# Gate/up seven-product units: two block sums made by accumulating transfers on GpSimd's queue

## What is computed

```python
def _swiglu_ffn(x, norm_g, w_gate, w_up, w_down):
    h = _rmsnorm(x, norm_g)
    return (jax.nn.silu(h @ w_gate) * (h @ w_up)) @ w_down
```

## Time and profile before

| what | value |
|---|---|
| runs | 2599.98 us median (2594.21 to 2600.82) |
| span of the profiled execution, first to last instruction | 2591.4 us, 8.6 us below the median of the runs |
| TensorE busy | 2562.1 us, 99% |
| VectorE busy | 1954.8 us, 75% |
| ScalarE busy | 1339.8 us, 52% |
| GpSimd busy | 189.2 us, 7% |
| moved by DMA | 548.21 MB, 212 GB/s over the span |
| TensorE's granted clock | 0.999 of full speed |

### The profile page before, as it was taken

How to read it: one execution, slowest core, us unless ns; L and a number is a source line. 1 busy time by engine, 2 the same in 40 slices (tenths; PEclk the granted TensorE clock), 3 DMA queues, 4 the chain that set the end, 5 groups by cost and what they waited for, 6 DMA issues and landing times.

```text
span 2591.4 us, 34224 instructions
## 1 busy us (share of the span) xinstructions
PE 2562.1 (99%) x13659; PEld 2103.4 (81%) x13659; DVE 1954.8 (75%) x2311; ACT 1339.8 (52%) x1568; POOL 189.2 (7%) x346
## 2 busy tenths in 40 slices
PE   8999999999999999999999999999999999999998
PEld 7888888888888777878788888888888888888887
DVE  6888888887767796959666766555668888888876
ACT  5555555555556366446455544433455455555554
POOL 2000000000000011010001112000100000000000
PEclk9999999999999999999999999999999999999999
DMA  6767676667776575656488779643767677766655
GB/s 213 232 210 242 210 236 218 217 208 228 216 210 195 184 228 159 179 165 181 146 280 257 252 245 281 201 155 130 239 190 230 222 226 225 227 219 218 210 201 175
DMA packets 278576, 548.21 MB, mean 212 GB/s; under 512 B 25020, under 2 KB 35424, under 8 KB 278032
## 3 DMA queue, kind: packets, MB, share of 16 engines
q1 hardware_dynamic: 253904, 478.60, 58.3%
q0 software_dynamic: 24192, 66.89, 8.8%
q10 hardware_dynamic: 320, 0.53, 0.1%
HBM read 508.15 MB, written 37.77 MB: 211 GB/s over the span
## 4 chain that ended last, share of the span: by engine, by line
PE 86%; DVE 8%; ACT 3%; DMA 2%; issue 1%; POOL 0%; SPq 0%; DVEq 0%; ACTq 0%; POOLq 0%
PE pp L794 14%; PE pp L795 14%; PE pp L796 14%; PE pp L415 11%; PE pp L416 11%; PE pp L417 11%; DVE wlo L376 2%; PE pa L794 1%; PE pb L796 1%; PE pb L795 1%; PE pb L794 1%; PE pa L795 1%; PE pa L796 1%; ACT whi L371 1%; DMA raw<-in_ffn_w_up 1%
## 5 line engine op out<-in xcount | busy, mean ns | idle before, releaser
L376 DVE TENSOR_TENSOR wlo<-raw,whi 128x1024 fp32r<-128x1024 f32 (+1 forms) x764 | 919.6, 1216 | 345.9 <-ACT whi L371 326.2
L371 ACT ACTIVATE whi<-raw 128x1024 fp32r<-128x1024 f32 (+1 forms) x764 | 798.0, 1053 | 626.5 <-PE pp L417 438.1
L794 PE MATMUL pp<-whi,xhi 128*128 128x512 f32 x1040 | 404.6, 389 | 0.0
L795 PE MATMUL pp<-whi,xlo 128*128 128x512 f32 x1040 | 404.6, 389 | 0.0
L796 PE MATMUL pp<-wlo,xhi 128*128 128x512 f32 x1040 | 404.6, 389 | 0.0
L415 PE MATMUL pp<-whi,xhi 128*128 128x512 f32 (+1 forms) x928 | 370.6, 399 | 0.7 <-DVE xlo L533 0.7
L417 PE MATMUL pp<-wlo,xhi 128*128 128x512 f32 (+1 forms) x928 | 359.6, 388 | 0.1
L416 PE MATMUL pp<-whi,xlo 128*128 128x512 f32 (+1 forms) x928 | 359.6, 387 | 0.0
L847 ACT ACTIVATE whi<-tw 128x1024 fp32r<-128x1024 f32 x124 | 131.6, 1062 | 276.3 <-PE pp L796 131.6
L794 PEld LDWEIGHTS pp<-whi,xhi 128*128 128x128 f32 x1040 | 195.2, 188 | 40.7
L796 PEld LDWEIGHTS pp<-wlo,xhi 128*128 128x128 f32 x1040 | 195.2, 188 | 40.6
(11 more groups left out here) (528 smaller groups left out, 3669.7 us busy)
## 6 DMA issues: line engine op xcount, KB each, us to landing
raw<-in_ffn_w_gate SPq DMA_DIRECT2D x176, 512.0 KB, 4.3
raw<-in_ffn_w_up SPq DMA_DIRECT2D x176, 512.0 KB, 4.7
raw<-in_ffn_w_down SPq DMA_DIRECT2D x176, 512.0 KB, 4.6
raw<-in_w_in SPq DMA_DIRECT2D x144, 512.0 KB, 4.3
hid_dram<-hid_t POOLq DMA_DIRECT2D x43, 512.0 KB, 5.0
xq<-hid_dram POOLq DMA_DIRECT2D x156, 128.0 KB, 3.8
raw<-in_w_lift SPq DMA_DIRECT2D x32, 512.0 KB, 5.9
raw<-in_w_out SPq DMA_DIRECT2D x32, 512.0 KB, 5.1
```

Of the source, the lines that this page charges most:

```text
L371: nc.scalar.activation(whi[:, s, :, 0:width], raw[:, r % RING, :, 0:width], ACT.Copy).then_inc(whi_ready, 1)
L376: nc.vector.tensor_tensor(wlo[:, s, :, 0:width], raw[:, r % RING, :, 0:width], whi[:, s, :, 0:width].bitcast(F32), ALU.subtract).then_inc( ...
L794: nc.tensor.matmul(out, a_hi, whi[:, s, block, :], start=start, stop=False)
L795: nc.tensor.matmul(out, a_lo, whi[:, s, block, :], start=False, stop=False)
```

## The change

For 38 of the 40 gate/up units (all but the first unit of chunk 1 in each block) VectorE's instruction for tw0 and tw1 goes. In its place SP loads B11 and B22 once more, straight into `tw` (two transfers of 256 KB), and GpSimd's queue then adds B12 to both by two accumulating transfers from DRAM (256 KB each). SP's two loads stand behind the load of slot t = 0 (first unit) or t = 4 (second unit) and wait until the `wlo` made from the old tw0 and tw1 is written. GpSimd's two transfers stand ahead of the `turn_out` of the same chunk. ScalarE and VectorE wait for the transfers' semaphore where they waited for the sum. To have semaphores for it, the small vectors at the start all count on one semaphore.

```diff
+OUTER_BEHIND = (0, 4)
...
+def outer_moved(i, u):
+
+    return (i, u) != (SEVEN[0], GU_UNITS[0])
...
+            def outer_load(i, u):
+
+                before = gu[2 * i]["pair"]["units"][u - 1] if u > 0 else gu[2 * i - 2]["pair"]["units"][-1]
+                j = GU_UNITS[u]
+                sp.wait_ge(wlo_ready, before[1] + 2)
+                for m, (w, k) in enumerate(((w_gate, 0), (w_up, 1))):
+                    sp.dma_start(tw[:, m, :], w[(j * SK + k) * P:(j * SK + k + 1) * P, i * CW:(i + 1) * CW]).then_inc(sem("outer_loaded"), 16)
...
                 for t, (pr, j, _, r) in enumerate(pair["plain"]):
                     load_slot(sp, rows_of(*(a if pr is pair["a"] else b)(j)), r)
+                    if chunk is not None and t in OUTER_BEHIND and outer_moved(chunk, GU_UNITS[OUTER_BEHIND.index(t)]):
+                        outer_load(chunk, OUTER_BEHIND.index(t))
...
-        def hidden_turns(pool, tag):
+        def outer_sum(pool, n, w_up):
+
+            _, i, u = OUTER[n]
+            j = GU_UNITS[u]
+            pool.wait_ge(sem("outer_loaded"), 32 * n + 32)
+            rows = slice(j * SK * P, j * SK * P + P)
+            for m in range(2):
+                nc.gpsimd.dma_start(tw[:, m, :], w_up[rows, i * CW:(i + 1) * CW], accum_op=ALU.add).then_inc(sem("outer_summed"), 16)
+
+        def hidden_turns(pool, tag, w_up):
             pool.wait_ge(sem("sums_ready"), SUMS[tag, "x"])
             for i in range(NFC):
+                for u in range(len(GU_UNITS)):
+                    if (tag, i + 1, u) in OUTER:
+                        outer_sum(pool, outer_of(tag, i + 1, u), w_up)
                 hidden_out(pool, tag, i)
...
             act.wait_ge(*loaded(r))
             hi(w, whi[:, w % RING, :, :], raw[:, r % RING, :, :])
-            act.wait_ge(sem("sums_ready"), SUMS[*mark, j, 1])
+            if summed is None:
+                act.wait_ge(sem("sums_ready"), SUMS[*mark, j, 1])
+            else:
+                act.wait_ge(sem("outer_summed"), 32 * summed + 32)
             hi(w + 1, whi[:, (w + 1) % RING, :, :], tw[:, 0:2, :])
...
-            v.tensor_tensor(tw[:, 0:2, :], blocks[:, b11:b22 + 1:3, :], blocks[:, b12:b12 + 1, :].to_broadcast([P, 2, CW]),
-                            ALU.add).then_inc(sem("sums_ready"), 1)
+            if summed is None:
+                v.tensor_tensor(tw[:, 0:2, :], blocks[:, b11:b22 + 1:3, :], blocks[:, b12:b12 + 1, :].to_broadcast([P, 2, CW]),
+                                ALU.add).then_inc(sem("sums_ready"), 1)
             lo(w, wlo[:, w % RING, :, :], raw[:, r % RING, :, :], whi[:, w % RING, :, :])
-            dve.wait_ge(sem("sums_ready"), SUMS[*mark, j, 1])
+            if summed is None:
+                dve.wait_ge(sem("sums_ready"), SUMS[*mark, j, 1])
+            else:
+                dve.wait_ge(sem("outer_summed"), 32 * summed + 32)
             v.tensor_tensor(tw[:, 2, :], tw[:, 0, :], blocks[:, b22, :], ALU.add).then_inc(sem("sums_ready"), 1)
...
-            pe.wait_ge(PRM_LOADED[g], 16 * sum(r // P == g for r in PRM.values() if r > 0))
+            pe.wait_ge(vectors_loaded, VECTORS)
```

More of the change, by code:

```diff
@@ L238, in count_marks @@
             for u in GU_UNITS:
-                sums += [(tag, "gu", i, u, step) for step in (1, 2, 3)]
+                sums += [(tag, "gu", i, u, step) for step in ((2, 3) if outer_moved(i, u) else (1, 2, 3))]
             acts += [(tag, "gu", i, "copied"), (tag, "gu", i, "gate")]
@@ L332, in build @@
         X_LOADED = [sem(f"x_loaded{c}") for c in range(NDC)]
-        PRM_LOADED = [sem(f"prm_loaded{g}") for g in range(2)]
+        vectors_loaded, VECTORS = sem("vectors_loaded"), 16 * (len(prm_sources(A)) + 1)
         rstd_ready, ident_ready = sem("rstd_ready"), sem("ident_ready")
@@ L630, in x_load, with outer_of @@
             sp.dma_start(h[:, :, cols], A["x"][0].rearrange("(t p) d -> p t d", p=P)[:, :, cols]).then_inc(X_LOADED[c], 16)
+        OUTER = [(tag, i, u) for tag in ("f1", "f2") for i in SEVEN for u in range(len(GU_UNITS)) if outer_moved(i, GU_UNITS[u])]
+        def outer_of(tag, i, u):
+            return OUTER.index((tag, i, u)) if (tag, i, u) in OUTER else None
         def ffn_load(sp, tag, w_gate, w_up, w_down):
@@ L636, in rows_of, with pair_load @@
                 return w[j * SK * P:(j + 1) * SK * P, c * CW:(c + 1) * CW].rearrange("(k p) n -> p k n", p=P)
-            def pair_load(pair, a, b):
+            def outer_load(i, u):
[4 more added lines that the diff above has]
+                    sp.dma_start(tw[:, m, :], w[(j * SK + k) * P:(j * SK + k + 1) * P, i * CW:(i + 1) * CW]).then_inc(sem("outer_loaded"), 16)
+            def pair_load(pair, a, b, chunk=None):
                 for t, (pr, j, _, r) in enumerate(pair["plain"]):
                     load_slot(sp, rows_of(*(a if pr is pair["a"] else b)(j)), r)
+                    if chunk is not None and t in OUTER_BEHIND and outer_moved(chunk, GU_UNITS[OUTER_BEHIND.index(t)]):
+                        outer_load(chunk, OUTER_BEHIND.index(t))
                     if t in pair["after"]:
@@ L656, in ffn_load @@
             for i in SEVEN:
-                pair_load(gu[2 * i]["pair"], lambda j: (w_gate, j, i), lambda j: (w_up, j, i))
+                pair_load(gu[2 * i]["pair"], lambda j: (w_gate, j, i), lambda j: (w_up, j, i), i)
             for q in range(NDC // 2):
@@ L839, in unit_pe, with unit_act @@
             product(e21, x(1, A_SECOND), (w + 3) % RING, 1, False, last).then_inc(slot_used, 1)
-        def unit_act(act, pair, n, mark):
+        def unit_act(act, pair, n, mark, summed=None):
             j, w, r = pair["units"][n]
@@ L856, in unit_act, with unit_dve @@
             hi(w + 3, whi[:, (w + 3) % RING, :, :], tw[:, 2:4, :])
-        def unit_dve(dve, pair, n, mark, between=None):
+        def unit_dve(dve, pair, n, mark, between=None, summed=None):
             v = nc.vector
@@ L972, in ffn_act @@
                     if t in GU_AFTER:
-                        unit_act(act, pair, GU_AFTER.index(t), (tag, "gu", i))
+                        n = GU_AFTER.index(t)
+                        unit_act(act, pair, n, (tag, "gu", i), summed=outer_of(tag, i, n))
                     if t == pair["na"]:
@@ L1067, in ffn_dve @@
                             dve.wait_ge(sem("banks_free"), BANKS[tag, "x"])
-                        unit_dve(dve, pair, n, (tag, "gu", i), between=(lambda: gated(i - 1)) if n == 0 else None)
+                        unit_dve(dve, pair, n, (tag, "gu", i), between=(lambda: gated(i - 1)) if n == 0 else None, summed=outer_of(tag, i, n))
                     if t == pair["na"] + 2:
@@ L1489, in aux_dve @@
             dve.wait_ge(sem("aux_turned"), 1)
-            dve.wait_ge(sem("gdn_loaded"), 32)
+            dve.wait_ge(vectors_loaded, VECTORS)
             v_.tensor_copy(beta_t[0:GHV, :], pa[0:GHV, 3, :]).then_inc(sem("aux_parts"), 1)
@@ L1528, in aux_act @@
             split_hi(act, first, 7)
-            act.wait_ge(sem("gdn_loaded"), 32)
+            act.wait_ge(vectors_loaded, VECTORS)
             link(act, nc.scalar.activation(nal, nal, ACT.Exp))
@@ L2660, in _ @@
                     if r // P == half and r > 0:
-                        g.dma_start(nat[r % P:r % P + m, half, 0:src.shape[-1]], src).then_inc(PRM_LOADED[half], 16)
+                        g.dma_start(nat[r % P:r % P + m, half, 0:src.shape[-1]], src).then_inc(vectors_loaded, 16)
             for cell, name in ((dtb, "gdn_dt_bias"), (nal, "gdn_a_log")):
-                g.dma_start(cell, A[name][0].rearrange("(g m) -> g m", m=1)).then_inc(sem("gdn_loaded"), 16)
+                g.dma_start(cell, A[name][0].rearrange("(g m) -> g m", m=1)).then_inc(vectors_loaded, 16)
             link(pool, g.memset(ones[:, :], 1.0))
@@ L2679, in _ @@
             g.memset(scanmask[:, :].rearrange("p (c t) -> p c t", t=C)[:, :, 0:1], 0.0).then_inc(consts_ready, 1)
-            hidden_turns(pool, "f1")
+            hidden_turns(pool, "f1", A["ffn1_w_up"][0])
             chunks_out(pool, "mixnorm", range(NDC - 1))
@@ L2791, in _ @@
             chunks_out(pool, "f2norm", range(NDC - 1))
-            hidden_turns(pool, "f2")
+            hidden_turns(pool, "f2", A["ffn2_w_up"][0])
             pool.wait_ge(slot_used, prods["f2dn"][0]["done"])
```

## The result

The changed kernel takes 2685.7 us (median of 4 runs, 2673.68 to 2686.77) against 2600.0 us before: a ratio of 1.0328, 95% interval 1.0314 to 1.0343. It is slower, as forecast, but by almost five times the 18 us, and outside the range. The profiled execution took 2685.4 us with a span of 2683.6 us, so only 1.8 us lie around a span. Most of the 8.6 us between the span before and its median was thus the scatter of the runs, and the spans exaggerate the loss a little (92 us).

A forecast was written before the change was run, and what follows sets the result against it. TensorE sets the pace in the gate/up stages. 0 gained at VectorE and 18 us lost at second units on a 2591.4 us span gave 2609.4; 8.6 more for runs: 2618 us (2608 to 2635; 8 in 10: 2596 to 2650).

The forecast's parts named there:

- VectorE's sum is worth nothing on the path: Gate/up units: removing 46.6 us of VectorE instructions, which lie under TensorE's work, gains nothing, at most 1.2 us.
- the 1.1 us as a credit for the second unit: Second units: slot 4's load is issued 1.1 us earlier, at 403.0, by the time VectorE gained in the first unit.
- The time of the sums in second units: Second units: outer loads land at 408.7, sums at 414.3 at a copy's price or, likelier, 417.3 at twice that.
- The price of twice a copy: GpSimd's accumulating transfers: block in tw and block from DRAM must both be read, so 3.0 us more than a copy.
- The 5.3 us from the sums to the fourth slot: Second units: whi, wlo, tw3, whi and wlo take 5.3 us, so sums must land by 416.4 for TensorE at 421.70.
- The second units, 20 times 0.9 = 18 us: Sums landing at 417.3 make TensorE wait 0.9 us in each of 20 second units; later plain slots finish in time.
- heavy rival: DMA engines become the bound, sums 2.0 us late, 20 x 2.0 = 40 us: 2640 us or more; chance 0.18.
- First units. Cost 0, and little in hand at the double price: First units: sums land by 436.4 or 439.4, while VectorE's own sum ended at 439.47; cost 0.
- GpSimd's other work: The turn_out behind the sums: store and loads land up to 3 us later, covered by 4.7 us; cost 0.
- The small vectors and SP's wait: Shared semaphore at the start, covered by over 20 us, and SP's wait for the old tw0 and tw1's wlo: 0.
- Bytes and share: DMA engines: about 40 MB more bytes, their share in gate/up stages rising from 0.71 to between 0.85 and 0.93.
- once or twice a copy: GpSimd's sums landing 5 us (copy) or 8 us (double) after issue: no difference, chance 0.38, or 8 to 35 us lost, 0.40.

The follow-up runs named there:

- experiment 1: Changed kernel without tw0 and tw1 in the 38 units (no VectorE sum, reload, accumulating transfer or wait); ratio 1.0001 against the kernel before.
- experiments 4 to 7: The change's transfers go into an unread block, no engine waits for sums; against kernel before, with VectorE's sum 1.0229 (accumulating), 1.0169 (copies); without it 1.0089, 1.0022.
- experiment 10: Changed kernel with only the 18 first units moved: ratio 1.0065, 17 us, against the kernel before; with only the 20 second units moved: 1.0287, 75 us.
- with copies: Changed kernel with plain copies in place of the accumulating transfers, waits kept; ratio 1.0079, 20 us, against the kernel before.
- the chain of four: Changed kernel, reload and transfers cut to 64 of 512 columns, four GpSimd transfers each behind the last's landing; ratio 1.0827, 215 us, against the kernel before.
- for three: Changed kernel, reload and transfers cut to 64 of 512 columns, three GpSimd transfers each behind the last's landing; ratio 1.0472, 123 us, against the kernel before.
- for two: Changed kernel, reload and transfers cut to 64 of 512 columns, two GpSimd transfers each behind the last's landing; ratio 1.0073, 19 us, against the kernel before.

## Why the prediction was wrong, step by step

**VectorE's sum is worth nothing on the path:** right, and shown alone (experiment 1). But the text took the 1.1 us as a credit for the second unit. That credit needs the first unit to be on time, and it was not. Under late loads VectorE's time has a price of 1 us a unit (experiments 4 to 7), and the change spent it on covering part of its own damage.

**The time of the sums in second units:** right. The text had them 13.4 us after the second outer load's issue (403.9 to 417.3), the trace has 13.5 (345.70 to 359.15), and 13.3 in the mean of all 20. The price of twice a copy held: 1.8 times the engine time. The 5.3 us from the sums to the fourth slot are 359.17 to 364.50 in the trace.

**The second units, 20 times 0.9 = 18 us:** the term that failed most. Alone they cost 75 us, 3.7 us a pair (experiment 10). Inside the unit the loss is about 2 us (1.67 us of waits in the pair shown, and about 0.3 us more at each of the two stops); the text had 2.0 us for the case without the credit, in its heavy rival. The rest comes behind the unit, where the text stopped counting. It let a late unit cost what TensorE waits inside it, as the plain slots behind it "finish in time", and compared only the engines' working time for that. The late unit also lets go of its `raw` buffers late, and the next first unit's up block is issued 2.3 us later.

**"First units. Cost 0, and little in hand at the double price":** failed as well, 17 us alone, and more beside late second units. The sums landed there as foreseen (12.7 us in the mean against 13.4). What the text compared them with was VectorE's old sum, and it never carried the bytes over to the load that stands behind them. The up block, 3.8 us on its way in the mean of such units before, was 6.0 us on its way (378.94 to 384.98), and TensorE waited 1.98 us. Leaving this out also set the price of the heavy rival, 40 us, too low by half: it counted a loss in second units only. Its condition, up blocks over 1.5 us later, was the one that held.

**GpSimd's other work:** the text had issues of 0.55 us; an accumulating one took 1.04 us, and the store behind it took 9.7 us to land where it took 5.0. The four loads were issued from 361.37 on and ScalarE read them at 370.92 without a wait, so cost 0 held.

**The small vectors and SP's wait:** cost 0, as said; among SP's waits there is none for the outer sums.

**Bytes and share:** 588.07 MB, 40 MB more, as said. The share of 0.79 lies below the 0.85 to 0.93 that was forecast, since a pair takes longer.

The chances were spread by one question, once or twice a copy. The case that came true went through the other one, what else a late unit holds up. No run tried that path alone (a late second unit whose buffers come free in time), so its share of the 86 us is read from the traces only. The direction, slower, was right, and for a right reason, the late sums of second units; the size was not.

## What to carry to other kernels

Here work was taken from an engine that had time to spare and given to the DMA engines; the gain was nil and the price was the landing time of a chain of transfers. In such a case write down by when each must have landed, and check the transfers that come behind it, and the buffers that a late user lets go late, with the same care as the moved one. An average share of 0.7 says little where loads come in bursts; look for the stretch in which the engines stand idle, and start the transfer there, if need be with a block of its own. The time that an engine has in hand is a stock against lateness and not waste: here it was worth 0 with loads on time and 1 us a unit with loads late.

## What was not expected of the hardware

The transfer with `accum_op` took 1.8 times the engine time of a copy of the same bytes (113 against 62 us). It also went in more packets: 35136 on this queue after the change against 30272 with copies, for the same 86.82 MB. The Trainium skill (Collectives: The Full Stack, Why ReduceScatter is half of AllGather) says that an adding transfer is slowed by its two source reads and not by the addition. Two reads would make it about twice a copy, and 1.8 is near that; that the reads are the reason, no run here shows. An estimate by the rule of the Trainium skill on GpSimd's transfers (DMA: Bandwidth & Descriptors, Anatomy of one DMA — SWDGE (gpsimd) path) is 2.6 us for 256 KB. The trace doesn't agree; it has far more for these, which come in twos and beside SP's loads (all of them, KB each, median us from issue to landing):

```profile
tw<-in_ffn_w_up POOLq DMA_DIRECT2D x76, 256.0 KB, 6.7
```

TensorE's clock fell in the kernel with the chain of four, and not after the change. In order of stretches of 3 us:

```profile
295.00:298.00 3.00, 1.59 (x8) 0.97 (x6) 0.00 (x0) 0.00 (x0) 0.77 (x2) 1.00 0.06 11
298.00:301.00 3.00, 0.00 (x0) 0.00 (x0) 1.59 (x2) 1.58 (x2) 0.54 (x1) 0.60 0.27 97
301.00:304.00 3.00, 2.62 (x6) 2.13 (x7) 2.48 (x4) 2.04 (x3) 1.54 (x3) 0.50 0.31 101
304.00:307.00 3.00, 3.00 (x11) 2.34 (x11) 2.64 (x3) 1.47 (x2) 0.66 (x2) 0.76 0.92 276
```

TensorE stood still from about 297 to past 301, and the granted clock went to 0.50, the lower level of 1.2 GHz. It was still there when TensorE worked again: 6 matmuls in the stretch from 301, where 14 or 15 are usual. Over this stage the clock was 0.92 for the chain of four, 0.98 for three and 1.00 for two. So the losses of 5.7 and 3.2 us a unit hold some of it, and the slope of one us for each us late is an upper reading, as is the estimate of 43 us made with it.
